# Window-attention heads: softmax scaled after the value product instead of before it, with the value product's operands exchanged

## What is computed

```python
def windowed_gqa_sink_attention(q, k, v, sink, pos, is_real):
    ...
        s_band = jnp.einsum('bqhgd,bkhd->bhgqk', qi, kb).astype(jnp.float32) * scale
        s_band = jnp.where(mask, s_band, NEG_INF)
        s_meta = jnp.einsum('bqhgd,bmhd->bhgqm', qi, k_meta).astype(jnp.float32) * scale
        s_sink = jnp.broadcast_to(sink_g[None, :, :, None, None], s_meta.shape[:-1] + (1,))
        p = jax.nn.softmax(jnp.concatenate([s_band, s_meta, s_sink], axis=-1), axis=-1)
        ...
        return (jnp.einsum('bhgqk,bkhd->bqhgd', p_band, vb)
                + jnp.einsum('bhgqm,bmhd->bqhgd', p_meta, v_meta))
```

## Time and profile before

| | |
|---|---|
| median of 3 runs | 996.38 us (995.86 to 997.63) |
| the profiled execution | 996.38 us, span 994.3 us |
| PE busy | 971.6 us, 98% |
| PEld busy | 879.8 us, 88% |
| DVE busy | 692.3 us, 70% |
| ACT busy | 539.8 us, 54% |
| POOL busy | 126.3 us, 13% |

### The profile page before, as it was taken

One profiled execution on the slowest core, in us unless ns is written; L12 is line 12 of the kernel. 1 busy time (PEld: TensorE's weight loads), 2 busy tenths in 40 slices (PEclk: granted clock), 3 DMA queues, 4 the chain that ended last, 5 costly groups with the idle time before them and its releaser, 6 DMA issues.

```text
span 994.3 us, 16734 instructions
## 1 busy us (share of the span) xinstructions
PE 971.6 (98%) x6780; PEld 879.8 (88%) x6780; DVE 692.3 (70%) x1288; ACT 539.8 (54%) x1039; POOL 126.3 (13%) x137
## 2 busy tenths in 40 slices
PE   8999999999999999999999999999899999999997
PEld 7988898888999988888989989888799998888886
DVE  6887676776477676767666778966665477767675
ACT  7776767664446644444355885544444364444443
POOL 2212222211002000000000139601100000000001
PEclk9999999999999999999999999999999999999999
DMA  9533333333348555555657542201352364555541
GB/s 321 181 128 128 128 128 128 128 128 121 137 157 262 197 177 204 176 205 174 208 172 247 212 128 86 85 1 43 128 169 86 107 212 171 199 182 197 183 169 42
DMA packets 126107, 154.97 MB, mean 156 GB/s; under 512 B 2728, under 2 KB 117680, under 8 KB 125648
## 3 DMA queue, kind: packets, MB, share of 16 engines
q1 hardware_dynamic: 123616, 142.91, 43.0%
q0 software_dynamic: 1952, 10.61, 3.0%
q10 hardware_dynamic: 464, 0.40, 0.2%
HBM read 150.76 MB, written 3.16 MB: 155 GB/s over the span
## 4 chain that ended last, share of the span: by engine, by line
PE 81%; DVE 10%; ACT 5%; DMA 1%; issue 1%; POOL 0%; POOLq 0%; DVEq 0%; ACTq 0%
PE ps L786 13%; PE ps L762 8%; PE ps L764 7%; PE ps L763 7%; PE ps L787 7%; PE ps L1068 5%; PE ps L1041 4%; PE ps L1042 4%; PE ps L1043 4%; PE ps L806 3%; DVE wlo L1313 3%; PE ps L748 3%; PE ps L807 3%; PE ps L808 3%; PE ps L907 2%; ACT whi L1954 2%
## 5 line engine op out<-in xcount | busy, mean ns | idle before, releaser
L1313 DVE TENSOR_TENSOR wlo<-raw,whi 128x1024 fp32r<-128x1024 f32 x268 | 325.9, 1232 | 170.4 <-ACT whi L1954 169.8
L1954 ACT ACTIVATE whi<-raw 128x1024 fp32r<-128x1024 f32 x268 | 274.5, 1050 | 146.8 <-PE ps L787 53.8
L786 PE MATMUL ps<-R1b,whi 128*128 128x512 f32 x576 | 201.8, 393 | 0.0
L762 PE MATMUL ps<-R1b,whi 128*128 128x256 f32 (+1 forms) x592 | 173.3, 293 | 0.8 <-DVE wlo L1313 0.8
L764 PE MATMUL ps<-R1b,wlo 128*128 128x256 f32 (+1 forms) x592 | 167.6, 283 | 0.0
L763 PE MATMUL ps<-R1b,whi 128*128 128x256 f32 (+1 forms) x592 | 167.5, 283 | 0.0
L787 PE MATMUL ps<-R1b,wlo 128*128 128x256 f32 x576 | 161.4, 280 | 0.0
L786 PEld LDWEIGHTS ps<-R1b,whi 128*128 128x128 f32 x576 | 108.1, 188 | 24.7 <-issue 0.5
L762 PEld LDWEIGHTS ps<-R1b,whi 128*128 128x128 f32 x592 | 111.5, 188 | 13.1 <-issue 10.6
L763 PEld LDWEIGHTS ps<-R1b,whi 128*128 128x128 f32 x592 | 111.5, 188 | 0.4 <-issue 0.2
L764 PEld LDWEIGHTS ps<-R1b,wlo 128*128 128x128 f32 x592 | 111.8, 189 | 0.0
(11 more groups left out here) (298 smaller groups left out, 2017.4 us busy)
## 6 DMA issues: line engine op xcount, KB each, us to landing
raw<-in_w_in SPq DMA_DIRECT2D x35, 1024.0 KB, 5.1
raw<-in_w_ffn_in SPq DMA_DIRECT2D x22, 1024.0 KB, 5.1
raw<-in_w_ffn_out SPq DMA_DIRECT2D x11, 1024.0 KB, 5.4
raw<-in_w_gate SPq DMA_DIRECT2D x11, 1024.0 KB, 5.1
raw<-in_w_up SPq DMA_DIRECT2D x11, 1024.0 KB, 5.3
raw<-in_w_down SPq DMA_DIRECT2D x11, 1024.0 KB, 5.4
raw<-in_w_out SPq DMA_DIRECT2D x8, 1024.0 KB, 5.1
raw<-in_w_xkv SPq DMA_DIRECT2D x8, 1024.0 KB, 5.8
```

Source lines behind the costliest of these rows:

```text
L762: e.matmul(o, hi[:, kt, c], R[0][:, kt, 0:n], start=kt == 0, stop=False)
L786: e.matmul(B[:, :].rearrange("p (a n) -> p a n", a=2), hi[:, kt, c], R[2][:, :, kt, 0:256], start=kt == 0, stop=False)
L1313: e.tensor_tensor(half_of(wlo[i % HL], i, k), half_of(raw[i % RAW], i, k), f32(half_of(whi[i % HL], i, k)), SUB).then_inc(lo_split(i, (i, k)))
L1954: return e.activation(o, i, f, **kw)
```

## The change

The matrices of exponentials are transposed unscaled. The step n is gone: sum, reciprocal and POOL's gathering stand in p0, which moves from step 4 to step 3 of the head. In v the transposed probabilities are stationary (128 columns) and the values moving (64 columns): eight matmuls per head instead of four, and one meta matmul with 256 columns instead of two with 128. The result has queries on the partitions, so that DVE can scale it by the reciprocal with one 128x256 product out of PSUM into OSB. A new PE part of t turns it back with `turn_out`, and ACT and DVE then read O[:, 256:512]. The step t moves from side 0 to side 1 of step 6. The first head has v at 6 and t at 7.

```diff
-STAGES = {"swa": ((0, 1, "s0"), (1, 0, "x0"), (1, 1, "s1"), (2, 0, "x1"), (3, 0, "n"), (4, 1, "p0"), (4, 1, "p1"),
-                  (5, 1, "v"), (6, 0, "t")),
+STAGES = {"swa": ((0, 1, "s0"), (1, 0, "x0"), (1, 1, "s1"), (2, 0, "x1"), (3, 1, "p0"), (4, 1, "p1"), (5, 1, "v"),
+                  (6, 1, "t")),
...
+FIRST = {"p0": 3, "p1": 4, "v": 6, "t": 7}
...
@@ tensor, swa
-                        p.wait_ge(head_dve, ("p", x, 2 * t + h))
+                        p.wait_ge(head_act, ("exp", x, 2 * t + h))
...
-                    for t in range(2):
-                        e.matmul(O[:, 128 * t:128 * t + 128], VM[:, kv, 2 * t:2 * t + 2, :], MT, start=t == 0, stop=False)
-                    p.wait_ge(head_act, ("PT", x, 0))
-                    p.wait_ge(head_dve, ("PT", x, 1))
-                    for h in range(2):
-                        for kt in range(2):
-                            m = e.matmul(O[64 * h:64 * h + 64, 0:256], VA[:, kt, 64 * kv:64 * kv + 64],
-                                         PTS[:, :, 256 * h + 128 * kt:256 * h + 128 * kt + 128], start=False, stop=kt == 1)
+                    e.matmul(O[:, 0:256], MT, VM[:, kv, :, :], start=True, stop=False)
+                    for t in range(2):
+                        p.wait_ge(head_dve if t else head_act, ("PT", x, t))
+                        for h in range(2):
+                            c = 128 * t + 64 * h
+                            for kt in range(2):
+                                m = e.matmul(O[:, c:c + 64], PT[t][:, 256 * h + 128 * kt:256 * h + 128 * kt + 128],
+                                             VA[:, kt, 64 * kv:64 * kv + 64], start=False, stop=(t, h, kt) == (1, 1, 1))
                     m.then_inc(head_pe(("V", x)))
+                if part == "t":
+                    turn_out(x)
...
@@ vector, swa
-                if part == "n":
+                if part == "p0":
...
-                    d.wait_ge(head_dve, ("rec", x))
-                    for u in range(4):
-                        ts(e4[:, u, 0:NT], e4[:, u, 0:NT], mx[:, u:u + 1]).then_inc(head_dve(("p", x, u)))
...
+                if part == "v":
+                    d.wait_ge(head_pe, ("V", x))
+                    d.wait_ge(head_dve, ("rec", x))
+                    if x:
+                        d.wait_ge(head_pe, ("T", x - 1))
+                    e.tensor_tensor(OSB.rearrange("p (u n) -> p u n", u=4), ps("O", x)[:, 0:256].rearrange("p (u n) -> p u n", u=4),
+                                    mx[:, 0:4].unsqueeze(2).to_broadcast([128, 4, 64]), MUL).then_inc(
+                        head_dve(("osb", x, 0), ("osb", x, 1)))
                 if part == "t":
                     d.wait_ge(head_act, ("oh", x))
-                    e.tensor_tensor(R3a[1][:, g, :], ps("O", x)[:, 0:256], f32(R3a[0][:, g, :]), SUB).then_inc(
+                    e.tensor_tensor(R3a[1][:, g, :], ps("O", x)[:, 256:512], f32(R3a[0][:, g, :]), SUB).then_inc(
...
@@ scalar, swa
-                    a.wait_ge(head_pe, ("V", x))
-                    act(R3a[0][:, g, :], ps("O", x)[:, 0:256]).then_inc(head_act(("oh", x)))
+                    a.wait_ge(head_pe, ("T", x))
+                    act(R3a[0][:, g, :], ps("O", x)[:, 256:512]).then_inc(head_act(("oh", x)))
...
@@ gpsimd, swa
-                if part == "n":
+                if part == "p0":
...
-                    pool.wait_ge(head_dve, ("p", x, 3))
+                    pool.wait_ge(head_act, ("exp", x, 3))
```

More of the change, by code:

```diff
@@ L360, in schedule @@
     for (kind, h), first in zip(HEADS, STARTS):
-        at += [(first + k, side, (kind, h, part)) for k, side, part in STAGES[kind]]
+        late = FIRST if (kind, h) == HEADS[0] else {}
+        at += [(first + late.get(part, k), side, (kind, h, part)) for k, side, part in STAGES[kind]]
     bdf = crossed("featk", [(("bdf", u), "w_branch_diff", 256 * u) for u in range(4)], 0,
@@ L579, in program @@
         PT = [SC[:, 2176 + 512 * i:2688 + 512 * i] for i in range(2)]
-        PTS = SC[:, 2176:3200].rearrange("p (t n) -> p t n", t=2)
         MC, MT = SC[:, 3200:3328], SC[:, 3328:3456]
@@ L2067, in diff @@
                     a.wait_ge(head_pe, ("V", x))
-                    if h:
+                    if x:
                         a.wait_ge(head_pe, ("T", x - 1))
```

## The result

| | before | after |
|---|---|---|
| median, same chip, 4 runs each | 997.0 us (995.86 to 997.75) | 1003.9 us (1002.36 to 1005.89) |
| the profiled execution | 996.38 us, span 994.3 | 1004.01 us, span 1002.2 |
| ratio after to before | | 1.0072 (95%: 1.0050 to 1.0093) |

The change makes the kernel 0.7% slower. 1003.5 was predicted, with 1001.5 to 1006.5 as the range. Run again later beside another set of runs of the kernel before (median 998.0 us), the changed kernel had a median of 1004.7 us (1002.45 to 1005.65, 6 runs) and a ratio of 1.0071 (1.0057 to 1.0085). Beside the first four experiments one run of the kernel before took 1920.4 us; as the slow run it is in none of the ratios.

A forecast was written before the change was run, and what follows sets the result against it. The prediction took TensorE's own instruction queue as the bound: 996.4 us plus 5.3 for the new v and 1.8 for the transposes, nothing returned, gives 1003.5 us, range 1001.5 to 1006.5.

The forecast's parts named there:

- The bound: Window-attention heads, 45 to 165 us: TensorE busy 120.00 of 120.00 us, so its own instruction queue sets the time.
- v: Value product of each head: 2.23 us instead of 1.66 alone or 1.47 with scores, 5.3 us added over eight heads.
- The price of a pass: New v on TensorE: each 64-column f32 pass costs 0.112 us, set by the weight load, not the moving columns.
- The old pairing: Old v's value matmuls, two by two in the array's halves: 0.13 us a pass against 0.22 alone; the change undoes it.
- The transposes: Two new TensorE transposes in t turn the output back: 0.22 us a head, 1.8 us for eight heads.
- No stall: Score banks, heads 1 to 3: chain through ScalarE and VectorE has 1.3 us to spare; the stall rival had 0.08.
- VectorE's relief is worth nothing: Heads' stretch: 5 us less VectorE work returns nothing, since TensorE doesn't wait for it; the rival giving 998.5 had 0.03.
- The total: Whole kernel: 5.3 + 1.8 = 7.1 us added to TensorE's queue, nothing returned, 996.4 to 1003.5 us.
- Everything behind shifted by the same 7: Sign on TensorE: two transposes at 271.03 us move to about 278.1, and all behind them shifts by the same 7.

The follow-up runs named there:

- the product alone: Kernel before with only the exchanged value product, scaling and order as before, no transposes back: heads 242.64 us (+5.00), median 1003.7 us, ratio 1.0041.

## Why the prediction was right, point by point

- **The bound.** TensorE's queue sets the stage: right. It is busy in all 127.00 us, and 9.4 us taken from VectorE change nothing. The product that comes first on VectorE waits 14.4 us in all for TensorE, not the other way round. The reading of TensorE's waits was too short, though: beside the 6.2 us ahead of projection loads there are 3.1 ahead of score loads and the four waits on ScalarE, 1.5 us. All were there before the change as well, and they did not grow (4.7, 2.2 and 1.5 after it).
- **v.** Predicted 2.23 us, measured 2.22 alone. With scores it is 3.02 instead of 2.32 + 0.76 = 3.08. Together 4 x 0.56 + 4 x 0.70 = 5.0; predicted 5.3; the product alone measured 5.00. The prediction also kept the old split of four heads alone and four with scores, while its own change moves the first head beside scores: three at 2.22 and five at 2.17 less the old 12.5 give 5.0 too.
- **The price of a pass.** Taken as 0.112 from 8 and 128 columns on either side of 64: measured 0.1125 from eight and sixteen passes of 64, and 128 columns cost the same. This term carried the sum and the sign. That the weight load is what costs it was inferred and still is. (With 0.107 a pass the sum falls by 0.7 us, not by the 0.6 stated.)
- **The old pairing.** The advice of the Trainium skill (TensorEngine Tiling (Array Packing), When to Use Tiling) holds here: undoing it costs 0.56 to 0.70 us a head, though the pairs came to 0.13 us a pass against 0.22 alone, less than a factor of two.
- **The transposes.** 0.22 x 8 = 1.8, measured 1.74 by leaving them out. p0 and p1 in two places cost nothing seen.
- **No stall.** Right, and with the right margin: 1.3 us claimed, 1.25 read, 1.17 by delaying until it bit.
- **VectorE's relief is worth nothing.** Right, though its size was off: 5 us less were expected, 6.8 came in the stretch. The scalings were taken by their starts (1.09 us a head); leaving them out took 9.4 us of busy time, 1.18 a head. The product took 3.4 us, as the groups by form of the changed kernel show (busy us, mean ns | idle before it):

```profile
L1452 DVE TENSOR_TENSOR SC<-ps,st 128x256 f32<-128x256 f32 x8 | 3.4, 425 | 14.4 <-PE ps L945 14.4
```

  9.4 less 3.4 is 6.0; the other 0.8 isn't assigned.
- **The total.** The stage grew by 6.67, not 7.08: the product's 5.3 was 5.00, the turning's 1.8 was 1.74, and the whole is within 0.1 of their sum. "Everything behind shifted by the same 7" was wrong: there is no single shift. In the profiled execution it is 6.9 us up to the middle, 6.3 behind it and 7.9 at the end. That the median came out 0.4 us from the forecast is partly luck: the forecast starts from an execution without a clock drop (996.38), and the median of 1003.9 is one of executions with one. At equal mean clock the change costs about 6.3 us, as told above, so the predicted 7.1 was 0.8 too much: 0.4 too much in the stage and 0.6 given back behind it, less the 0.25 that this run had ahead of the heads.

**What gave 0.6 back.** TensorE has one wait near 590 us that its queue doesn't set. The same matmul in the timelines of the kernel before and of the changed one:

```profile
590.26 1.60 PE L753 MATMUL ps<-ca 128*128 128x128 f32 x12 [1.71 <-ACT SE L1954]
```

```profile
596.54 1.60 PE L755 MATMUL ps<-ca 128*128 128x128 f32 x12 [1.11 <-ACT SE L1963]
```

The matmuls just ahead of it start 6.9 us later than before, but it ends its wait only 6.3 later. The copy for which it waits hangs on VectorE, whose split and scalings there are 6.3 us later as well. VectorE's timeline, before and after, shows where that begins:

```profile
570.18 0.69 DVE L1664 TENSOR_TENSOR SC<-ps,F 128x512 f32<-128x512 f32 x1 [0.53 <-DMA kept_kv<-SC]
```

```profile
576.47 0.68 DVE L1673 TENSOR_TENSOR SC<-ps,F 128x512 f32<-128x512 f32 x1
```

Before, VectorE waits 0.53 us for a transfer that saves a buffer to memory (kept_kv) to end, since its next result goes into that buffer; in the changed kernel the transfer is through in time. The DMA views of the two kernels (KB, us from issue to landing):

```profile
kept_kv<-SC POOLq DMA_DIRECT2D x1, 2048.0 KB, 10.2
```

```profile
kept_kv<-SC POOLq DMA_DIRECT2D x1, 2048.0 KB, 9.0
```

From the transfer's issue to VectorE's start it is 10.22 us before and 9.61 after, 0.61 less, which is the 0.6. All nine executions whose heads are 4.9 us or more longer than before have 9.6 and no wait there. The other five wait 0.19 to 0.53 us and have 9.9 to 10.2, and their middles are longer by as much (316.1 and 316.4 us, or 317.6 to 317.8 with a drop, against 315.8 or 317.3). Why the transfer lands sooner in the later kernels is open.

## What to carry to other kernels

When the stage is TensorE's own queue, count passes: behind 128x128 weights an f32 matmul is two passes of 0.112 us each up to 128 moving columns, so turning a 64-wide product round doubles its passes for nothing, and the lighter VectorE is no return. Before moving a vector step ahead of a bank's last reader, add up the chain and compare it with the time at which TensorE asks; it can be measured by repeating one instruction in the chain until the stage grows. Put a reader that frees a bank ahead of a long split, not behind. When executions of one program spread in steps, compare those of equal mean clock: differences of 0.7 us show there that medians hide.

## What the runs showed of the hardware

- A group of sixteen f32 passes behind 128x128 weights takes 1.71 us with 64 columns and 1.70 with 128. Two passes of 256 columns take 0.43 us.
- The old v costs 1.66 us alone and 1.47 with the 64-row scores behind it; the new one 2.22 and 2.17 (3.02 less 0.85). Where the old v, on half of the array's columns, stands next to scores, on half of its rows, 0.19 us are saved; where the new v does, whose passes use all of it, only 0.05.
- Behind a pause of 1.5 to 1.9 us in TensorE, or some shorter ones, stood in some executions 3.4 us at the lower clock level, a loss of 1.5 to 1.6 us. Near 660 us the same program shows the drop once and once not.
- The same transfer of 2 MB took 10.2 us from issue to landing in one kernel and 9.0 in the other, where it stands 6.9 us later.
